# Hybrid encoder trunk on one core: the first differential exponential's scaling moves from VectorE to ScalarE, and the softmax reciprocals move ahead of the weight's low part

## What is computed

```
def diff_attention(h, w_in, q_norm, k_norm, lq1, lk1, lq2, lk2, sub_norm, lambda_init):
    proj = (h @ w_in).astype(f32)
    q, k, v = jnp.split(proj, 3, axis=-1)
    ...
    lam = (jnp.exp(jnp.sum(lq1 * lk1)) - jnp.exp(jnp.sum(lq2 * lk2)) + lambda_init)
    def block(args):                      # one block of 128 queries
        ...
        s = jnp.einsum('bqhzd,bkhzd->bzhqk', qblk, k) + bias[None, None]
        p = jax.nn.softmax(s, axis=-1)
        attn = p[:, 0] - lam * p[:, 1]
        return jnp.einsum('bhqk,bkhe->bqhe', attn, v)
    ...
    o = rms_norm(o, sub_norm) * (1.0 - lambda_init)
    return o.reshape(bsz, L, DIFF_HEADS * DIFF_DV)
```

## Time and profile before

| | us |
|---|---|
| median of 3 runs (2362.08 to 2363.11) | 2362.84 |
| the profiled execution's own time | 2362.28 |
| its span in the profile | 2360.5 |
| PE busy in the span | 2345.7 |
| DVE busy | 1578.4 |
| ACT busy | 1199.6 |

### The profile page before, as it was taken

One profiled execution on the slowest core, in us unless ns is written; L12 is line 12 of the kernel. 1 busy time (PEld: TensorE's weight loads), 2 busy tenths in 40 slices (PEclk: granted clock), 3 DMA queues, 4 the chain that ended last, 5 costly groups with the idle time before them and its releaser, 6 DMA issues.

```text
span 2360.5 us, 34797 instructions
## 1 busy us (share of the span) xinstructions
PE 2345.7 (99%) x13771; PEld 2011.3 (85%) x13771; DVE 1578.4 (67%) x2586; ACT 1199.6 (51%) x2123; POOL 0.2 (0%) x4
## 2 busy tenths in 40 slices
PE   9999999999999999999999999999999999999999
PEld 6888877888889888988888888888898898888888
DVE  8999668776687776665765548859985475433332
ACT  6334455555445565545564436647873453432432
POOL 0000000000000000000000000000000000000000
PEclk9999999999999999999999999999999999999999
DMA  5346533553224554445435233233234324333222
GB/s 209 95 105 180 209 111 106 165 207 116 72 90 149 194 187 135 137 134 161 134 106 169 84 98 123 90 107 99 93 108 152 116 81 131 111 97 98 98 98 90
DMA packets 117441, 297.93 MB, mean 126 GB/s; under 512 B 20000, under 2 KB 48416, under 8 KB 116000
## 3 DMA queue, kind: packets, MB, share of 16 engines
q1 hardware_dynamic: 108720, 271.98, 36.0%
q10 hardware_dynamic: 8560, 23.73, 3.2%
HBM read 267.48 MB, written 19.79 MB: 122 GB/s over the span
## 4 chain that ended last, share of the span: by engine, by line
PE 83%; DVE 6%; ACT 1%; issue 1%; ACTq 0%
PE ps L1663 62%; PE ps L1640 5%; PE ps L1686 3%; PE ps L1645 3%; PE ps L1757 2%; PE ps L1788 1%; DVE wlo L1613 1%; DVE region_S L2271 1%; PE ps L1848 1%; PE ps L1821 1%; DVE vtmp L2250 0%; PE ps L1772 0%; PE ps L2296 0%; PE ps L2363 0%; PE ps L1702 0%
## 5 line engine op out<-in xcount | busy, mean ns | idle before, releaser
L1608 ACT ACTIVATE whi<-wraw 128x1024 fp32r<-128x1024 f32 x430 | 451.9, 1052 | 205.5 <-PE ps L1663 125.6
L1613 DVE TENSOR_TENSOR wlo<-wraw,whi 128x1024 fp32r<-128x1024 f32 x430 | 522.8, 1218 | 6.9 <-ACT whi L1608 6.7
L1663 PE MATMUL ps<-in_hP,whi 128*128 128x512 f32 x1272 | 504.8, 397 | 1.7 <-DVE in_lP L2183 0.9
L1663 PE MATMUL ps<-in_hP,wlo 128*128 128x512 f32 x1272 | 495.7, 390 | 0.0
L1663 PE MATMUL ps<-in_lP,whi 128*128 128x512 f32 x1272 | 495.4, 389 | 0.0
L1663 PE MATMUL ps<-hid_P,whi 128*128 128x512 f32 x1008 | 310.8, 390 | 0.0
L1663 PEld LDWEIGHTS ps<-in_hP,whi 128*128 128x128 f32 x1272 | 238.9, 188 | 53.8 <-issue 2.1
L1663 PEld LDWEIGHTS ps<-in_hP,wlo 128*128 128x128 f32 x1272 | 238.8, 188 | 50.6
L1663 PEld LDWEIGHTS ps<-in_lP,whi 128*128 128x128 f32 x1272 | 239.0, 188 | 49.4 <-issue 1.4
L2105 DVE TENSOR_TENSOR x<-ps,x 128x256 f32<-128x256 f32 (+1 forms) x191 | 106.2, 556 | 251.0 <-PE ps L1663 248.9
L1663 PE MATMUL ps<-in_S,whi 128*128 128x256 f32 x1408 | 260.9, 287 | 0.0
(11 more groups left out here) (564 smaller groups left out, 3784.9 us busy)
## 6 DMA issues: line engine op xcount, KB each, us to landing
wraw<-wt SPq DMA_DIRECT2D x432, 512.0 KB, 3.5
wraw<-wt ACTq DMA_DIRECT2D x16, 512.0 KB, 4.2
k_scratch<-region_P SPq DMA_DIRECT2D x16, 256.0 KB, 3.2
v_scratch<-vtmp SPq DMA_DIRECT2D x32, 128.0 KB, 3.4
x<-x_in SPq DMA_DIRECT2D x4, 768.0 KB, 6.6
x<-x_in SPq DMA_DIRECT2D x2, 1536.0 KB, 7.0
mix_mem<-mem_in ACTq DMA_DIRECT2D x1, 2048.0 KB, 15.9
region_S<-k_scratch ACTq DMA_DIRECT2D x2, 1024.0 KB, 6.9
```

Source lines behind the costliest of these rows:

```text
L1608: nc.scalar.activation(whi[:, (n + 3) % NHI, :, :], wraw[:, ws(n), :, :], ACT.Copy).then_inc(wh.sem, 1)
L1613: nc.vector.tensor_tensor(wlo[:, ws(n), :, :], wraw[:, ws(n), :, :], whi[:, (n + 3) % NHI, :, :].bitcast(F32), ALU.subtract).then_inc(wr.s ...
L1663: last = nc.tensor.matmul(ps[:, bank(m), 0:N[prod.g]], w_[:, k, :], x_[:, k, :], start=(k == 0 and j == 0), stop=(k == KT - 1 and j == 2))
```

## The change

ACT gets one new operation in each step: the first exponential times its reciprocal, in place (`act_diff_scale`), behind `high` and ahead of the tile's own operations. It waits for the reciprocals. DVE computes the reciprocals in a new function, `dve_diff_reciprocal`, called right behind the maximum and so ahead of `low`, and multiplies the second reciprocal (one column) by minus lambda. The former pass over the second exponential (line 2245) is gone; the last pass now multiplies the second exponential by that column and adds the first, which ACT has scaled, and waits for ACT's signal. Two semaphores of the first part of the program are reused for the two signals.

```diff
+            def act_diff_scale(a, d_, t):
+                if 0 <= t - 1 < d_.n:
+                    q_ = d_.b + t - 1
+                    a.wait_ge(reciprocals.sem, reciprocals.at(d_.done + t))
+                    nc.scalar.activation(scb[d_.g][:, q_ % 2, 0, :], scb[d_.g][:, q_ % 2, 0, :], ACT.Copy, scale=st[:, q_ % 2, 6:7])\
+                        .then_inc(scaled.sem, 1)
...
+            def dve_diff_reciprocal(v, d_, t):
+                if 0 <= t - 1 < d_.n:
+                    q_ = d_.b + t - 1
+                    s_ = st[:, q_ % 2, :]
+                    v.wait_ge(expd.sem, q_ + 1)
+                    nc.vector.reciprocal(s_[:, 6:8], s_[:, 4:6]).then_inc(reciprocals.sem, 1)
+                    v.wait_ge(reciprocals.sem, reciprocals.at(d_.done + t))
+                    dve_chain(nc.vector.tensor_tensor(s_[:, 7:8], s_[:, 7:8], lam[:, 5:6], ALU.mult))
...
             def dve_diff_prob(v, d_, t):
...
-                    v.wait_ge(expd.sem, q_ + 1)
-                    dve_chain(nc.vector.reciprocal(s_[:, 6:8], s_[:, 4:6]))
-                    dve_chain(nc.vector.tensor_scalar(e_[:, 1, :], e_[:, 1, :], s_[:, 7:8], lam[:, 5:6], ALU.mult, ALU.mult))
...
+                    v.wait_ge(scaled.sem, scaled.at(d_.done + t))
                     v.wait_ge(tr.sem, max(d_.b, q_ - 1))
-                    nc.vector.scalar_tensor_tensor(vtmp[:, q_ % 2, 0:N[g]], e_[:, 0, :], s_[:, 6:7], e_[:, 1, :], ALU.mult, ALU.add)\
+                    nc.vector.scalar_tensor_tensor(vtmp[:, q_ % 2, 0:N[g]], e_[:, 1, :], s_[:, 7:8], e_[:, 0, :], ALU.mult, ALU.add)\
                         .then_inc(prob.sem, 1)
...
                             if t[2] + NHI - 1 < NT:
                                 high(a, t[2] + NHI - 1)
+                            for step in steps:
+                                if step[0] == "diff":
+                                    act_diff_scale(a, step[1], step[3])
                             if not q_first(t, steps):
                                 act_tile(a, t)
...
                             elif step[0] == "diff":
                                 dve_diff_max(v, step[1], step[3])
+                                dve_diff_reciprocal(v, step[1], step[3])
```

More of the change, by code:

```diff
@@ L242, in mixer_in @@
             ud, t_v, vt_done, vt_ready, cl_ready, lag_done, rt_copied, rt_ready, m_loaded = (sig(f"m_{n}") for n in (
-                "ud", "tv", "vtd", "vtr", "cl", "lag_then_kq_stacked", "rtc", "rtr", "ml"))
+                "ud", "tv", "vtd", "vtr", "cl", "lag_then_kq_stacked", "rtc_then_reciprocals", "rtr_then_scaled", "ml"))
             bu_done, st_ready, y_done, yg_ready = (sig(f"m_{n}") for n in ("bu", "st", "yd", "ygr"))
@@ L990, in mixer_in, with trunk_tail @@
             lag_done.take(NB)
-            return mem[:, :, :], ymem[:, :], mem_reload, zeros, setup, lag_done
-        def trunk_tail(mem, ymem, mem_reload, kq_high_d, kq_low_d, kq_stacked):
+            rt_copied.take(NB)
+            rt_ready.take(NB)
+            return mem[:, :, :], ymem[:, :], mem_reload, zeros, setup, lag_done, rt_copied, rt_ready
+        def trunk_tail(mem, ymem, mem_reload, kq_high_d, kq_low_d, kq_stacked, reciprocals, scaled):
             NHI = 4
@@ L1197, in __init__ @@
                         s_.take(self.n)
-                    self.ob = ofree.base
+                    self.ob, self.done = ofree.base, DH * BL["S"] if g == "P" else 0
                     self.hi, self.lo = kq_high_d.take(DH), kq_low_d.take(DH)
@@ L2701, in _ @@
                                 high(a, t[2] + NHI - 1)
+                            for step in steps:
+                                if step[0] == "diff":
+                                    act_diff_scale(a, step[1], step[3])
                             if not q_first(t, steps):
                                 act_tile(a, t)
+                        for step in steps:
+                            if step[0] == "diff" and t is None:
+                                act_diff_scale(a, step[1], step[3])
                         if before is not None:
```

## The result

The changed kernel takes 2371.2 us (median of 6 runs, 2370.8 to 2371.7), the kernel before 2363.0 in the same comparison: ratio 1.0036, 95% interval 1.0026 to 1.0046, 8.2 us slower. Forecast were 2369.5, so 6.7 slower; the time lies in the stated range (2361.0 to 2372.0), and 0.5 above the narrower one that the forecast gave for its own case (2367.3 to 2370.7).

What follows compares the result with a forecast made beforehand. PE bounds the kernel, busy 99%; only P's attention can lose, in DVE-ACT loops: 0.60 + 3 x 0.76 + 2 x 2.07 = 7.02, less 0.33, 6.7 us late, so 2369.5 us (chance 0.62); range 2361.0 to 2372.0, its own case 2367.3 to 2370.7.

Steps and rivals of the forecast that it cites:

- S's attention costs nothing: S's attention: PE never waits there, so the added ACT pass and DVE wait cost nothing; without that cover at most 10 us.
- DVE's relief: DVE in P's attention: a 0.58 us pass removed, a 0.19 column product added; net gain 0.39 a slot, 1.56 a head.
- the floor: P's attention: PE's 21.89 us a head stays as the lower limit once DVE's own work falls to 20.73.
- the first rival: P's attention: DVE's saving decides and PE is the bound; PE's idle 2.00 us goes, giving 2360.8 us; chance 0.10.
- The scaling's price: ACT's added pass over 128x512: 0.71 us taken, between bounds 0.63 and 0.71; the next operation starts after 0.61.
- The column product: DVE's added single-column product: 0.16 us long, 0.19 to the next start, taken from the nearest row, a two-column reciprocal.
- The heads: P's attention: from 22.29 us a head to 23.05 with down tiles (0.76 more) and 24.36 with up tiles (2.07 more).
- the sum: P's attention: step lengths added round one closed DVE-ACT loop between successive high parts of the output: 23.05 or 24.36 us.
- third rival: P's attention: each of about eight hand-overs a loop costs 0.1 us more; six heads lose 4.8 more, 2374; chance 0.09.
- The first stretch: P's attention, from exponentials at 1614.08 to the first high part: 1626.71 instead of 1626.11, 0.60 us late.
- The end: Past the last high part followed, no head is stacked; PE is the bound again and carries the delay to the end.
- PE's idle time: P's attention, 1614 to 1738: a sign of being right, PE's idle time growing from 2 to about 9 us.

## Why the prediction was right, step by step

**S's attention costs nothing:** right; the run with S alone shows it.

**DVE's relief:** the size was right, the floor was not. With the relief alone heads fall to 21.64 us and the kernel gains 3.2. The forecast took PE's 21.89 a head for its own work and so 2360.8 for the first rival; so some 0.25 us of that busy time was no work that PE needs. The relief is real, and the waits of the move alone cost more than it gives.

**The scaling's price:** 0.71 was taken; the trace of after has 0.708 as the median of 32 (0.704 to 0.727), and 0.495 for 256 columns. (By the Trainium skill, page "ScalarE: Activation LUTs", section "What ACT_TABLE_LOAD costs", with its term for a per-partition operand, the estimate is 0.71; the trace agrees.) The column product takes 0.16 and 0.19 to the next start, as taken.

**The heads:** 23.04, 23.06 and 23.06 us with down tiles for 23.05; 24.36 for 24.36 in one of the two with up tiles. The eight up tiles lie two, four and two in three heads; in the first of these they stand in its last two slots, and it pays no more than heads without any: in this order only the first two slots behind a high part count, as in the sum. In the orders of the experiments the last two count too (22.93 against 21.94 with the squares first).

**The hand-overs cost more (third rival):** no. In the changed kernel eight hand-overs a loop are within 0.02 us of the sum. So close an agreement is not what such sums gave elsewhere: in the orders of the experiments they missed single heads by up to 1.4 us.

**What was mis-sized,** against the 6.7 us that PE was to be late. At the sum matmuls of the sixth head, where the forecast ends, PE is 7.73 late (1729.14 before, 1736.87 after), the 0.33 less than at the high part (8.06) that the forecast had. The 1.04 too much are two terms:

- The first stretch, 1.14 for 0.60. The forecast started from exponentials at 1614.08 as if nothing before them had moved; they start at 1614.60. At step 1, in the slot with the first stacking copy, the last pass waits 0.92 for the scaling, the next maximum comes late, and PE waits 0.48 for it (1591.89). The forecast had that very wait, but only inside the heads.
- One head with up tiles, 24.85 for 24.36: 0.49. PE's wait of 2.19 us in it was followed by half the clock; with PE kept busy the head took 0.55 less.

**The end:** the forecast let the delay stand from there. At the last two sum matmuls of the attention PE is 7.94 and 8.59 late: the last heads lose 0.86 more. In the window behind 1737.50 0.35 of it is idle time of PE. The experiments say which part of the change it belongs to. From the sixth to the eighth head's sum matmul the kernel before takes 37.25 us (from 1729.14) and the changed kernel 38.11 (from 1736.87); with the move and no scaling it is 38.08 (from 1731.03), with neither move nor scaling 37.25 (1726.29 to 1763.54). So the last heads lose by the move, whose wait for the squares' low part stands in both kernels, and not by the scaling.

```profile
1774.98 0.47 PE L1857 MATMUL ps<-sq_hP,ones_r 128*128 128x512 f32 x1 [0.21 <-DVE sq_lP L2256]
...
1769.11 0.47 PE L1857 MATMUL ps<-sq_hP,ones_r 128*128 128x512 f32 x1 [0.23 <-DVE sq_lP L2256]
```

So 6.7 + 0.5 + 0.5 + 0.9 = 8.6.

**PE's idle time** was to grow to about 9 us between 1614 and 1738; it grew to 5.54. The same delay stands in two places: PE's busy time grew by 3.5 us with no more work, and 6.5 us at half the clock are some 3.3 of that.

## What to carry to other kernels

When two engines pass an item to and fro, add up the closed loop from one mark to the same mark a period later, operation by operation, for each kind of neighbour work: here that gave the heads of the changed kernel to 0.02 us, where the busy shares (DVE and ACT both idle for over 14% of that stretch) don't show that anything is lost. In other orders of the same operations such sums were up to 1.4 us a head off, so check the heads one by one and not only the total. Moving a pass from a full engine to one with room pays only if the full engine then doesn't wait for it; here the relief of 3.2 us cost 5.7 in the order it needed and 5.7 in ACT's scaling, its pass and its hand-over together, which no run takes apart. Start such a sum at the first item, not at the first regular period, and follow it to the last.

## What the runs showed of the hardware

A single wait of TensorE of 2.19 us, between stretches in which it was full, was followed by about 6.5 us at 0.50 of its clock (1.2 of 2.4 GHz). With seven matmuls put into that wait, a gap of 0.44 remained and the clock stayed at 1.00. The length of the wait alone doesn't decide it: in that same execution a wait of 2.18 us one head later left the clock at 1.00; with the squares' low part first, PE waits 2.36 us ahead of 1698.34 and the clock stays at 1.00 in every stretch of 2 us around it; with the scaling done twice, waits of 2.93 and 2.94 are followed by some 4 us of slow clock, and of three waits of 1.62 one is followed by as much (0.50 from 1652 to 1654) and two by none. By the two heads compared, 3.3 us of longer matmuls cost 0.55 in the changed kernel, so most of them were covered; by the sum of the prediction ACT's queue is the path there.
